# Eight of 22 activation tiles of the third down projection in seven block products, between its output groups

## The reference

```python
def swiglu(h, w_gate, w_up, w_down):
    return (jax.nn.silu(h @ w_gate) * (h @ w_up)) @ w_down
...
    for i in range(DEPTH):
        j = i // 2
        h = h + 0.5 * swiglu(rms_norm(h, norms[i, 0]), ffn_w_gate[i, 0], ffn_w_up[i, 0], ffn_w_down[i, 0])
        hn = rms_norm(h, norms[i, 1])
        ...
        h = h + mix
        h = h + 0.5 * swiglu(rms_norm(h, norms[i, 2]), ffn_w_gate[i, 1], ffn_w_up[i, 1], ffn_w_down[i, 1])
```

## Time and profile before

| | us |
|---|---|
| median of 3 runs | 1891.66 (1890.3 to 1891.82) |
| the profiled execution | 1889.01 |
| its span, first to last instruction | 1887.2 |
| PE busy | 1858.4 (98%) |
| DVE busy | 1354.8 (72%) |
| ACT busy | 895.7 (47%) |
| POOL busy | 260.9 (14%) |
| mean granted clock of PE | 0.998 |

### The profile page before, as it was taken

How to read it: one execution, slowest core, us unless ns; L and a number is a source line. 1 busy time by engine, 2 the same in 40 slices (tenths; PEclk the granted TensorE clock), 3 DMA queues, 4 the chain that set the end, 5 groups by cost and what they waited for, 6 DMA issues and landing times.

```text
span 1887.2 us, 31448 instructions
## 1 busy us (share of the span) xinstructions
PE 1858.4 (98%) x11418; PEld 1615.1 (86%) x11418; DVE 1354.8 (72%) x1983; ACT 895.7 (47%) x1509; POOL 260.9 (14%) x204
## 2 busy tenths in 40 slices
PE   8999999999999999999999999999989999999998
PEld 6899988777799998887899998877658899998886
DVE  8788788774988874357888864269984988874355
ACT  7455542245555563234455553244563655554222
POOL 0000001312100000234000001073243100000225
PEclk9999999999999999999999999999999999999999
DMA  5233333332233333323333332232101233333321
GB/s 180 90 112 101 99 106 105 96 100 86 78 98 95 109 112 111 111 67 101 100 92 99 111 123 96 93 109 68 57 1 46 91 100 99 111 105 118 105 74 56
DMA packets 56753, 179.88 MB, mean 95 GB/s; under 512 B 12144, under 2 KB 12144, under 8 KB 56656
## 3 DMA queue, kind: packets, MB, share of 16 engines
q1 hardware_dynamic: 54656, 173.69, 29.7%
q0 software_dynamic: 928, 3.02, 0.5%
q10 hardware_dynamic: 1088, 2.10, 0.3%
HBM read 175.04 MB, written 3.15 MB: 94 GB/s over the span
## 4 chain that ended last, share of the span: by engine, by line
PE 87%; DVE 9%; ACT 2%; POOL 1%; issue 1%; DMA 0%; DVEq 0%; SPq 0%; POOLq 0%; ACTq 0%
PE ps L2314 36%; PE ps L2276 26%; PE ps L2258 17%; PE ps L2762 2%; PE ps L2425 1%; DVE work L1256 1%; DVE sm L1280 1%; DVE stat L1254 1%; POOL sumsq L1556 1%; DVE x_lo L441 1%; ACT prob L1998 0%; PE ps L2476 0%; PE ps L2288 0%; DVE sm L1299 0%; PE ps L2711 0%
## 5 line engine op out<-in xcount | busy, mean ns | idle before, releaser
L389 DVE TENSOR_TENSOR w_lo<-raw,w_hi 128x1024 fp32r<-128x1024 f32 x174 | 231.6, 1340 | 217.0 <-ACT w_hi L381 216.3
L381 ACT ACTIVATE w_hi<-raw 128x1024 fp32r<-128x1024 f32 x186 | 194.2, 1054 | 293.9 <-PE ps L2276 248.7
L2314 PE MATMUL ps<-xs_hi,w_hi 128*128 128x256 f32 x1088 | 308.2, 283 | 0.5
L2314 PE MATMUL ps<-xs_lo,w_hi 128*128 128x256 f32 x1088 | 307.9, 283 | 0.0
L2314 PE MATMUL ps<-xs_hi,w_lo 128*128 128x256 f32 x1088 | 307.9, 283 | 0.0
L2276 PE MATMUL ps<-act_hi,w_hi 128*128 (+1 forms) x720 | 280.5, 390 | 0.0
L2276 PE MATMUL ps<-act_lo,w_hi 128*128 (+1 forms) x720 | 280.1, 389 | 0.0
L2276 PE MATMUL ps<-act_hi,w_lo 128*128 (+1 forms) x720 | 280.1, 389 | 0.0
L2258 PE MATMUL ps<-x_hi,w_hi 128*128 128x512 f32 x640 | 257.5, 402 | 8.5 <-ACT w_hi L381 7.2
L2258 PE MATMUL ps<-x_hi,w_lo 128*128 128x512 f32 x640 | 250.2, 391 | 0.0
L2258 PE MATMUL ps<-x_lo,w_hi 128*128 128x512 f32 x640 | 249.8, 390 | 0.0
(11 more groups left out here) (412 smaller groups left out, 3545.5 us busy)
## 6 DMA issues: line engine op xcount, KB each, us to landing
raw<-in_weights SPq DMA_DIRECT2D x322, 512.0 KB, 3.6
h<-in_xT ACTq DMA_DIRECT2D x4, 512.0 KB, 6.4
out<-result SPq DMA_DIRECT2D x4, 512.0 KB, 3.0
p_raw<-in_pT POOLq DMA_DIRECT2D x2, 512.0 KB, 4.2
scratch_u<-u_sc SPq DMA_DIRECT2D x1, 512.0 KB, 6.6
u_grp<-scratch_u SPq DMA_DIRECT2D x1, 512.0 KB, 4.1
scratch_y<-y_grp SPq DMA_DIRECT2D x2, 256.0 KB, 3.1
y_ch<-scratch_y SPq DMA_DIRECT2D x1, 512.0 KB, 3.6
```

Source lines behind the costliest of these rows:

```text
L381: act.activation(w_hi[:, slot], raw[:, slot], ACT.Copy).then_inc(hi_ready, 1)
L389: dve.tensor_tensor(w_lo[:, slot], raw[:, slot], w_hi[:, slot].bitcast(F32), SUB)\
L2314: last = pe.matmul(ps[:, bank, 0:HALF], w[:, at, cols], x[:, k], start=(start and k == 0 and part == 0), stop=(stop and k == KH - 1 and pa ...
```

## The change

Only the third block's down stage (`f = 2`) changes. Activation tiles 0 to 7 go through seven block products, as in the up stage; tiles 8 to 21 go on as before. The stage has three parts: seven plain chunks for output group 0 (tiles 8 to 21), four mixed tiles (each two output tiles, activation tiles 0 to 7, 84 matmuls of 256 columns), and seven plain chunks for output group 1. New are:

- four block sums of the activations (`b_sum`), made by DVE within the last three up tiles, and their split in the plain half (`block_hi`, `block_lo`, with three unmixed corners);
- sums of weight blocks per mixed tile, four instructions of 512 columns, and their splits;
- `copied` (ACT) and `added` (DVE), which bring the partial products to the residual `h` directly, in six additions per tile;
- mixed weight chunks that SP gathers from the same weights by two transfers of 256 KB each, in pieces of 512 bytes.

`part_sum` is packed to make room, DVE's loop over up tiles ends one turn earlier in all four blocks (its last turn is written out), and POOL's first square waits for the last half.

```diff
+MIXED_DOWN = (2,)
...
+DOWN_STEPS = (NF - KD) // 2
+DOWN_MIXED = DOWN_STEPS
+DOWN_LAST = DOWN_STEPS + KD
...
             def last_tile(i, b):
 
-                act_low(dve, f, 0)
-                act_low(dve, f, 1)
+                if f in MIXED_DOWN:
+                    block_sum(3)
+                else:
+                    act_low(dve, f, 0)
+                    act_low(dve, f, 1)
...
+            fast_tile(NF // 2 - 2, 0)
+            if f in MIXED_DOWN:
+                block_sum(0)
+            fast_tile(NF // 2 - 2, 1)
+            if f in MIXED_DOWN:
+                block_sum(2)
             fast_tile(NF // 2 - 1, 0)
+            if f in MIXED_DOWN:
+                block_sum(1)
             last_tile(NF // 2 - 1, 1)
...
+        def mixed_down_act(act, n, first, after=None):
...
+            for j in range(DOWN_STEPS):
+                if AHEAD + j < DOWN_STEPS:
+                    split_hi(act, first, AHEAD + j)
+                act_high(act, f, KD + 2 * j, first)
+                act_high(act, f, KD + 2 * j + 1, first)
+                if j in (0, 1):
+                    block_hi(2 * j)
+                    block_hi(2 * j + 1)
...
+            for c in range(GROUP):
+                more = c + 1 < GROUP
+                copied(c, 0)
+                copied(c, 1)
+                copied(c, 2)
+                if more:
+                    sum_hi(c + 1, "T4")
+                    sum_hi(c + 1, "T2")
+                    own_hi(c + 1, 0)
...
+                copied(c, 3)
+                if more:
+                    sum_hi(c + 1, "T13")
+                    own_hi(c + 1, 1)
...
+            def mixed_tile(c):
...
+                pe.wait_ge(split_ready, start + 2 * c + 1)
...
+                product(first_bank, at["B11"], parts[4], True, False, mixed["product"])
+                pe.wait_ge(mixed["t_ready"], 3 * g + (3 if c else 1))
+                product(right_bank, at["T1"], parts[0], True, False, mixed["product"])
+                pe.wait_ge(mixed["t_ready"], 3 * g + 3)
+                pe.wait_ge(mixed["copied"], 4 * g + 1)
+                product(first_bank, at["T2"], parts[1], False, False, mixed["product"])
+                product(left_bank, at["B21"], parts[5], True, True, mixed["product"])
+                pe.wait_ge(mixed["copied"], 4 * g + 3)
+                product(first_bank, at["T3"], parts[2], False, False, mixed["product"])
+                pe.wait_ge(split_ready, start + 2 * c + 2)
+                product(right_bank, at["B22"], parts[3], False, True, chunk_used)
+                pe.wait_ge(mixed["copied"], 4 * g + 4)
+                product(first_bank, at["T4"], parts[6], False, True, chunk_used)
+
+            for m in range(DOWN_STEPS):
+                ready(pe, m)
+                down_chunk(pe, first, m, 0, m == 0, m == DOWN_STEPS - 1,
+                           static(act_hi, m), static(act_lo, m))
+            for c in range(GROUP):
+                mixed_tile(c)
+            pe.wait_ge(mixed["late"], 4 * u + 2)
+            for m in range(DOWN_STEPS):
+                down_chunk(pe, first, DOWN_LAST + m, 1, m == 0, m == DOWN_STEPS - 1,
+                           static(act_hi, m), static(act_lo, m))
```

More of the change, by code:

```diff
@@ L68 @@
 CHUNKS = STARTS[-1]
+DOWN_STARTS = tuple(STARTS[i] + FFN_UP for i in (0, 3, 5, 8))
 TWO_PI = (6.28125, 0.0019340515, 1.2556659e-06)
@@ L334, in encoder @@
             "t_ready", "product", "copied")}
+        mixed = {n: sem(f"mixed_{n}") for n in (
+            "sums", "b_hi", "b_ready", "w_sums", "t_hi", "t_ready", "product", "copied", "added",
+            "late", "h_part")}
         tab = sem("tab")
@@ L371, in turn_of, with loads_of @@
             return i + (first + j) // SLOTS
+        def loads_of(first, j, i=0):
+            twice = sum(first + j >= DOWN_STARTS[f] + DOWN_LAST for f in MIXED_DOWN)
+            return i * 16 + (turn_of(first, j) * 16 + 16 + 32 * twice)
         def split_hi(act, first, j, i=0):
@@ L1810, in last_tile @@
             def last_tile(i, b):
-                act_high(act, f, 0)
-                act_high(act, f, 1)
+                if f not in MIXED_DOWN:
+                    act_high(act, f, 0)
+                    act_high(act, f, 1)
                 copy_part(i, b, 0)
@@ L2399, in down_pe, with mixed_down_pe, static, product @@
                     m += 1
+        def mixed_down_pe(pe, f, n, first, ready):
+            u = MIXED_BEFORE[f]
+            start = first + DOWN_MIXED
+            def static(a, m):
+                at = KD + 2 * m
+                return lambda row: a[:, (at + row) * T:(at + row + 1) * T]
+            def product(bank, at, x, begin, end_, done):
+                for k in range(KH):
+                    cols = slice(k * P, (k + 1) * P)
+                    for part, (w, rhs) in enumerate(((wf_hi, x[0]), (wf_hi, x[1]), (wf_lo, x[0]))):
+                        last = pe.matmul(ps[:, bank, 0:HALF], w[:, at, cols], rhs[:, k],
+                                         start=(begin and k == 0 and part == 0),
+                                         stop=(end_ and k == KH - 1 and part == 2),
+                                         skip_group_check=True)
+                last.then_inc(done, 1)
+            def mixed_tile(c):
+                g = 4 * u + c
+                at = mixed_halves(start, c)
+                first_bank, left_bank, right_bank = mixed_banks(c)
+                parts = [(b_hi[o], b_lo[o]) for o in range(4)]
+                for rows, cols in ((slice(0, KH), slice(0, HALF)), (slice(KH, KD), slice(0, HALF)),
+                                   (slice(KH, KD), slice(HALF, T))):
+                    parts.append((acts_hi[:, rows, cols], acts_lo[:, rows, cols]))
+                pe.wait_ge(split_ready, start + 2 * c + 1)
+                if c == 0:
+                    pe.wait_ge(mixed["b_ready"], 7 * (u + 1))
+                if c == 1:
+                    pe.wait_ge(mixed["h_part"], GROUP * (u + 1))
+                if c > 1:
+                    pe.wait_ge(h_ready, tiles_before(n, 2 * c - 3))
+                product(first_bank, at["B11"], parts[4], True, False, mixed["product"])
[15 more added lines that the diff above has]
+                           static(act_hi, m), static(act_lo, m))
+            for c in range(GROUP):
+                mixed_tile(c)
[3 more added lines that the diff above has]
+                           static(act_hi, m), static(act_lo, m))
@@ L2405, in ready @@
             def ready(pe, m):
-                pe.wait_ge(ffn_sems["act_ready"], m * 2 + 2 + NF * f)
+                pe.wait_ge(ffn_sems["act_ready"], m * 2 + 2 + ACTS_BEFORE[f])
+            if f in MIXED_DOWN:
+                mixed_down_pe(pe, f, n + 1, first + FFN_UP, ready)
+                return
             down_pe(pe, first + FFN_UP, NF // 2, ready, between)
```

325 lines of the change are left out of this document (306 added, 19 removed).

## The result

The changed kernel takes 1894.36 us (median of 20, 1893.56 to 1896.89) against 1891.25 for the kernel before on the same chip (20 runs): +3.1 us, ratio 1.0018, 95% interval 1.0012 to 1.0025, so a real loss. The forecast was 1893.8 with 2.15 us of loss.

The account below looks back on a forecast made before the run. The prediction took PE to bound the kernel, busy 98% of the span. It summed -3.15 (matmuls), +4.0 (entry wait) and +1.3 (clock) to +2.15 us, so 1891.66 becomes 1893.8, range 1891 to 1897.5.

Parts of the forecast that it names:

- The likeliest case: Entry wait and clock fall outweigh the saved matmuls in the third down stage: +2.15 us, 1893.8; chance 0.55.
- the sum: Whole kernel: -3.15 + 4.0 + 1.3 = +2.15 us, median 1891.66 becoming 1893.8, +0.11%.
- the list of signs: Profile after: 4.0 us entry idle, clock low 3.4 us, matmuls in 38.1, 40.4 and 38.1 us, stage 121 to 122.
- term 3: Start of the down stage: the clock falls after the entry pause, matmuls run at half rate; +0.85 to +1.7, taken +1.3 us.
- Term 1: PE in the down stage: 192 matmuls of 512 columns go, 336 of 256 come; -3.15 us.
- Term 2: Entry into the down stage: PE waits for the act_lo of tiles 8 and 9; +4.0 us.
- The end of the stage: Last updates, x_lo and next projection keep their order; nothing added.
- The loads of 256 KB: Mixed weight chunks: two transfers each in 512-byte pieces, nearest rows 3.6 and 4.1 us, due about 10 us later; covered.
- The four block sums: DVE in the last three up tiles: 1.22 us each, covered by idle time; without that cover up to 0.5 us.
- Rival 1: Entry into the down stage: the clock stays up after the wait; +0.85 us, 1892.5; chance 0.12.
- rival 4: Entry into the down stage: no wait, the first pair of splits is ready anyway; 1888.5 us; chance 0.03.
- Rival 2: Mixed tiles: DVE becomes the bound, low part of T1/T3 late; +4.55 us, 1896.2; chance 0.24.

Follow-up runs that it names:

- experiment 2: Changed kernel with the first pair of activation splits (tiles 8 and 9) moved into the last up tile; 1888.96 us against 1890.78 before, ratio 0.9994.
- experiment 8: Changed kernel with early first splits and the old order of last updates, in the second, third and fourth blocks; 1881.13 us against 1891.10 before.
- kernel 7: Changed kernel with the first pair of splits in the last up tile and the old order of last updates; 1887.24 us against 1891.10 before.
- experiment 3: Changed kernel with four extra matmuls on PE, results unread, between the up and down stages; 1892.50 us against 1890.78 before.
- 4: Changed kernel with two more DVE additions of 1024 elements in each of the first three mixed tiles; 1899.68 us against 1890.78 before.
- 5: Changed kernel with only the high parts of tiles 8 and 9 moved into the last up tile; 1892.58 us against 1891.10 before.
- 6: Changed kernel with tile 3's low part of x put back between the updates of tiles 4 and 5; 1893.82 us against 1891.10 before.
- 9: Kernel before, with only tile 3's low part of x moved behind the last half's fifth chunk split; 1891.97 us against 1890.99 before.

## Why the prediction was right, and where not

The likeliest case came about and the time lies 0.6 us over the number, so the sum missed about 1 of 3.1 us; that the number came nearer is luck, since the kernel before ran 0.4 us faster here (1891.25) than in the runs the forecast started from (1891.66). The prediction called the change one that can't be told from none; 20 runs of each kernel told it. The stage took 122.44 us where 121 to 122 were given, and the first 168 matmuls 39.97 where the list of signs had 38.1, without the loss that term 3 put there. By its steps:

- **Term 1 (-3.15)** held: 3.18 in experiment 2, where nothing else stands in the stage, and three times over in experiment 8. Both rates from the earlier trace rows carried over; the estimate from the Trainium skill (TensorE: Matmul & The Clock Gate, "Wait — 56ns, not 53.3ns?"), 4.7, did not. The chain of kernel 7 shows it: 38.11 + 40.31 + 38.11 = 116.53 against 119.71.
- **Term 2 (+4.0)** measured 3.93, by the instructions it named. That it is the cause is shown by experiment 2.
- **Term 3 (+1.3, at most 1.7)** measured 1.86 (39.97 less 38.11). The mechanism was right (experiment 3: a busy PE keeps its clock), the size too small, for two reasons. The step that failed is "With a delay of 2.1 to 3.8 us it begins at 1111.4 to 1113.1": the fall came 5.2 us after PE stopped (1111.00 to 1116.21). So none of the low stretch lay in the pause, and all of it was paid for: 1.60 us by experiment 3 (39.97 less 38.37). The other 0.26 us come with a wait whatever the clock does, and no term had them. What the Trainium skill says of too long gaps (TensorE: Matmul & The Clock Gate, "HAM oscillation — how this bites in real kernels") agrees in part: the clock fell after each of the four idle pauses of 2.5 to 3.9 us at this entry (the changed kernel, 4, 5 and 6), but the next work did not always start cold. In the changed kernel it ran for 1.28 us at full clock before the fall (1114.93 to 1116.21).
- **The end of the stage** is what the prediction got wrong: "The end (last updates, x_lo, next projection) keeps its order." It didn't. One low part was moved out from between two updates; this was to be seen in the diff. It cost 1.05 us in the mixer (experiments 6, 7 and 9). The steps between are read from the traces, not each tried: the low part of tile 4 then starts together with POOL's sum (1231.24 and 1231.23) and takes 1.83 us, the last updates and weight splits slip, the second load with them, and it then runs beside POOL's five loads for longer; lam_vec, the last of them, is late, and all of POOL's work up to sm waits for it. But the late load is only about half of it. Counted from the next projection, POOL's multiplications begin 0.84 us later than before (18.36 against 17.52: 1251.52 less 1233.16, 1246.38 less 1228.86), and the last step of sm 1.58 us later (33.35 against 31.77: 1266.51 and 1260.63). The rest arises within the multiplications, in the kernel before and then in the changed one:

```profile
1253.02 1.56 POOL L1604 TENSOR_SCALAR w_uk<-w_uk,params 128x512 f32<-128x512 f32 x1
1254.56 2.99 POOL L1604 TENSOR_SCALAR w_uv<-w_uv,params 128x512 f32<-128x512 f32 x1
```

```profile
1258.28 3.61 POOL L1863 TENSOR_SCALAR w_uk<-w_uk,params 128x512 f32<-128x512 f32 x1
```

The one that starts beside DVE's pair of weight splits is the long one: before, the splits begin at 1253.84, behind w_uk; in the changed kernel at 1258.17, just ahead of it, and w_uv takes 1.56. Both kernels with the wait gone (6 and 7) have w_uk at 1.56 again, so the rows fit, but no run tries this step alone. Of the 1.58 us PE had 0.57 in hand (sm ended at 1261.91, PE came at 1262.48).

- **The sum**, made again with rows: -3.18 + 3.93 + 1.86 + 1.05 = +3.66, against 3.1 by the medians and 3.4 by the ratio (2.3 to 4.7).
- Nothing else cost PE time in the stage (-3.18 + 3.93 + 1.86 is its 2.61). The loads of 256 KB landed in 3.1 us. The four block sums delayed no matmul. Rival 1 and rival 4 are out by the rows of the result. Rival 2 did not come, by 0.85 us: the low part of T1 and T3 ends at 1165.40 and T1 begins at 1166.25 in the first mixed tile, where the walk gave 1 us.

Open is why the clock's fall comes at such different times behind a pause (below), and with it 0.7 us of what a run of this kernel takes, as the entries of the changed kernel and of 6 differ.

## What to carry to other kernels

When the order of products is changed, ask which operands the first ones need and make those in the stage ahead: here a saving of 3.2 us was paid back nearly twice by one pair of splits in the wrong place, and moving two lines on each engine won it back. Here a pause of TensorE between two busy stretches cost its length and some 1.8 us (once 2.6) for clock and restart, whether it was 2.5 or 3.9 us long; three of 1.6 us cost their length and some 0.26 us each. Read a diff for what it takes out of a sequence, also where the time it moves is idle: an instruction between two others may be what keeps one engine from running beside another, and here what that cost appeared some 36 us later (1231.24 to 1267.83).

## What the runs showed of the hardware

- The fall of the clock after a pause has no fixed delay. TensorE stopped at 1111.00, 1110.59 and 1110.95 in the changed kernel and in 5 and 6; the clock fell 5.2, 3.3 and about 2.0 us later, so in the first two PE was busy again, and in kernel 6 it still stood. It stayed at 0.50 for 3.4 us in the first two and 6.8 in kernel 6, whose windows are:

```profile
1112.50:1113.00 0.50, 0.00 (x0) 0.00 (x0) 0.50 (x1) 0.50 (x2) 0.00 (x0) 1.00 0.90 131
1113.00:1119.50 6.50, 4.62 (x11) 3.69 (x12) 5.06 (x7) 6.12 (x8) 0.00 (x0) 0.50 0.52 174
1119.50:1120.00 0.50, 0.50 (x2) 0.37 (x2) 0.50 (x2) 0.00 (x0) 0.00 (x0) 0.66 0.96 287
```

- Three pauses of 1.6 us, some 12 us apart, left the clock at 1.00 in kernel 4; one of 2.01 us was followed by a fall in the kernel before. A pause of 0.95 us at sm left the clock up in the changed kernel (its pair of matmuls took 1.12 us) and likewise in 3, 4, 5 and 9 (1.12 or 1.13), and in kernel 2 the clock was down behind the same pause (2.02 us for the pair): PE's lead of 2.28 us over the kernel before, late in the down stage (1215.70 against 1217.98), was a lag of 0.47 two sums further on (1265.00 against 1264.53).
- VectorE's low part of x (512 elements, two operands in SBUF) ends about 0.55 us after the GpSimd instruction beside which it starts, however much of that is left. In the changed kernel it starts with GpSimd's sum (1231.24 and 1231.23), which ends at 1232.52, and ends at 1233.07 (1.83 us). In the kernel before it starts at 1226.94 with 0.29 us of GpSimd's square left (1225.82 + 1.41 = 1227.23) and ends at 1227.77 (0.83 us):

```profile
1225.59 0.74 DVE L441 SCALAR_TENSOR_TENSOR x_lo<-h,gains,x_hi 128x512 fp32r<-128x512 f32 x1
```

```profile
1226.94 0.83 DVE L441 SCALAR_TENSOR_TENSOR x_lo<-h,gains,x_hi 128x512 fp32r<-128x512 f32 x1
```

```profile
1225.82 1.41 POOL L1552 TENSOR_TENSOR square<-h 128x512 f32<-128x512 f32 x1 [39.80 <-DVE h L730]
```

GpSimd is held up in turn: this square starts 0.23 us behind a low part (1225.59) and takes 1.41 us, where the same square of the changed kernel, with no low part beside it, takes 1.05 (1230.11). The Trainium skill (SBUF — State Buffer, "SBUF: two separate sides") has a rule for such a pair, that the one which starts second is blocked until the other is through; these traces agree, with either engine as the one that waits.
